# A hybrid encoder trunk on one core: transposes of queries and keys in a new sequence, the closing steps behind the branch, the last products of one output bank postponed

## The reference

```
for layer in range(2):
    hn = rms_norm(x, norm_mix_g[layer])
    z = hn @ w_in                       # x_rnn, y_gate, q, k, v, gates
    # branch 1: depthwise conv, gated linear scan forward and backward, times gelu(y_gate)
    # branch 2: 12 heads in 3 groups, dilated band attention, groups mixed by softmax
    x = x + (sigmoid(g0) * branch_lru + sigmoid(g1) * branch_att) @ w_out
    hn = rms_norm(x, norm_ffn_g[layer])
    if layer == 0: x = x + (silu(hn @ w_gate) * (hn @ w_up)) @ w_down
    else:          x = x + sum over the top 2 of 8 experts of share_e * swiglu_e(hn)
out = rms_norm(x, final_norm_g)
```

## Time and profile before

| | |
|---|---|
| median of 3 runs | 1567.9 us (1566.28 to 1568.82) |
| the profiled execution | 1565.57 us |
| its span, first to last instruction | 1563.8 us |
| PE, DVE, ACT busy | 98%, 53%, 30% of the span |
| DMA | 306 GB/s over the span |
| chain that ended last | PE 82%, ACT 8%, DVE 7%, issue 2% |

### The profile page before, as it was taken

The page is one execution under the profiler, slowest core; times in us unless marked ns, Lnnn a source line. Parts: engine busy times, 40 slices in busy tenths (PEclk is TensorE's granted clock), DMA queues, the critical chain, the costliest instruction groups (busy, mean ns, idle before and its releaser), DMA issues.

```text
span 1563.8 us, 28403 instructions
## 1 busy us (share of the span) xinstructions
PE 1526.8 (98%) x12112; PEld 889.5 (57%) x12112; DVE 822.7 (53%) x1766; ACT 471.7 (30%) x692; POOL 22.9 (1%) x37
## 2 busy tenths in 40 slices
PE   7998999999999989999999999999999999999997
PEld 6886788888888867853434434334334334343342
DVE  6777666555687776754533335336145234342262
ACT  5697655444456977420000000000000000000001
POOL 0000000000000000010000000000000000000000
PEclk9999999999999999999999999999999999999999
DMA  9543265555553433589999999999999999999992
GB/s 384 180 160 136 107 245 200 189 188 189 188 175 135 161 137 123 199 308 413 410 398 425 421 407 425 411 401 425 409 426 418 414 426 411 406 425 413 421 425 109
DMA packets 68354, 478.66 MB, mean 306 GB/s; under 512 B 7616, under 2 KB 7872, under 8 KB 12160
## 3 DMA queue, kind: packets, MB, share of 16 engines
q1 hardware_dynamic: 64480, 460.88, 73.7%
q0 software_dynamic: 3456, 15.72, 2.7%
q10 hardware_dynamic: 288, 0.19, 0.0%
HBM read 471.90 MB, written 4.85 MB: 305 GB/s over the span
## 4 chain that ended last, share of the span: by engine, by line
PE 82%; ACT 8%; DVE 7%; issue 2%; DMA 0%; DVEq 0%; SPq 0%; ACTq 0%
PE bank L1339 26%; PE turn L1354 12%; PE mid L1339 11%; PE turn L1360 6%; PE bank L1076 6%; PE bank L1080 6%; PE bank L1083 6%; ACT w_hi L535 2%; PE mid L1076 2%; PE mid L1083 2%; PE mid L1080 2%; DVE w_lo L542 2%; PE mid L1175 1%; ACT root L890 1%; ACT rg L902 1%
## 5 line engine op out<-in xcount | busy, mean ns | idle before, releaser
L1339 PE MATMUL bank<-wide,gT 128*32 128x512 f32 (+1 forms) x3952 | 423.6, 565 | 0.0
L542 DVE TENSOR_TENSOR w_lo<-raw,w_hi 128x1024 fp32r<-128x1024 f32 x202 | 245.3, 1223 | 142.1 <-ACT w_hi L535 140.0
L1339 PEld LDWEIGHTS bank<-wide,gT 128*32 128x32 f32 x3952 | 154.9, 110 | 245.3 <-issue 238.7
L535 ACT ACTIVATE w_hi<-raw 128x1024 fp32r<-128x1024 f32 x202 | 211.4, 1056 | 122.0 <-PE bank L1083 81.1
L1897 DVE STREAM_TRANSPOSE hT<-eh 32x128 f32<-32x128 f32 (+1 forms) x768 | 219.9, 286 | 24.1
L1354 PE MATMUL turn<-wide,hT 128*32 128x512 f32 x1792 | 215.8, 592 | 0.0
L1339 PE MATMUL mid<-wide,gT 128*32 128x256 f32 (+1 forms) x2048 | 192.0, 486 | 0.0
L1013 ACT ACTIVATE eh<-bank 128x512 f32<-128x512 f32 (+1 forms) x32 | 17.4, 544 | 534.6 <-PE bank L1339 306.3
L1076 PE MATMUL bank<-w_hi,a_hi 128*128 128x512 f32 (+1 forms) x608 | 165.7, 396 | 0.7 <-ACT a_hi L763 0.7
L1083 PE MATMUL bank<-w_lo,a_hi 128*128 128x512 f32 (+1 forms) x608 | 157.4, 383 | 2.1 <-DVE w_lo L542 2.1
L1080 PE MATMUL bank<-w_hi,a_lo 128*128 128x512 f32 (+1 forms) x608 | 157.7, 383 | 0.0
(11 more groups left out here) (254 smaller groups left out, 1165.4 us busy)
## 6 DMA issues: line engine op xcount, KB each, us to landing
wide<-in_stream SPq DMA_DIRECT2D x330, 1024.0 KB, 8.1
raw<-in_stream SPq DMA_DIRECT2D x106, 1024.0 KB, 4.8
wg<-in_gates POOLq DMA_DIRECT2D x2, 2048.0 KB, 10.3
table<-y_rows POOLq DMA_DIRECT2D x7, 384.0 KB, 7.8
gain<-in_norms POOLq DMA_DIRECT2D x4, 512.0 KB, 7.1
x<-in_x SPq DMA_DIRECT2D x2, 512.0 KB, 6.5
raw<-in_stream SPq DMA_DIRECT2D x2, 512.0 KB, 6.8
tokens<-xs POOLq DMA_DIRECT2D x1, 1024.0 KB, 5.4
```

The costliest lines, as they stand in the source:

```text
L535: nc.scalar.activation(w_hi[:, h % H, :], raw[:, part % R, lo:lo + HALF], ACT.Copy).then_inc(hi_ready, 1)
L542: nc.vector.tensor_tensor(w_lo[:, h % H, :], raw[:, part % R, lo:lo + HALF], w_hi[:, h % H, :].bitcast(F32), ALU.subtract).then_inc(lo_rea ...
L1339: ins = nc.tensor.matmul(bank_[strip(s_), 0:w], gT[:, kt, strip(t_)], w_c, start=kt == 0, stop=kt == KT - 1)
```

## The change

1. The `tq` steps run in the sequence 0, 1 / 4, 5 / 2, 3. ACT makes all six copies. Those of 0, 1, 4, 5 wait for the first half of the backward scan only, 2 and 3 for both.
2. `an` stands directly behind `am` (at 20.5 + i, before at 21 + i).
3. The two loads of the first norm's factors (`load_first_gain`) are issued by ACT, the first ahead of the identity and the second behind it; SP issued them before, between the loads of `x` and of the first weights.
4. In the last expert the last three output parts make all their products for `turn[0]` first; then `rows_done` is signalled, and their products for `turn[1]` follow. The strip of `turn[0]` (ACT) and `y_end` (DVE) wait for `rows_done`.
5. The last two products of `ENDS` take `yt` as float32; the steps for high and low words are gone.
6. The closing steps and the last norm stand behind the branch on ACT and DVE, once on each side of it.

```diff
-        at(19.5, ("tq", 2), ("tq", 3))
-        at(20, ("tq", 4), ("tq", 5), ("evac", ("g1", 0)))
+        at(19.5, ("tq", 4), ("tq", 5))
+        at(20, ("tq", 2), ("tq", 3), ("evac", ("g1", 0)))
         for i in range(PAIRS):
-            at(20.5 + i, ("as", i), ("am", i))
-            at(21 + i, ("an", i))
+            at(20.5 + i, ("as", i), ("am", i), ("an", i))
...
             load_x(0)
-            load_first_gain(0)
             sp.dma_start(raw[:, 0, 0:HALF], stream[0, :, 0:HALF]).then_inc(first_landed, 16)
             sp.dma_start(raw[:, 0, HALF:PART], stream[0, :, HALF:PART]).then_inc(landed[0], 16)
             load_x(1)
-            load_first_gain(1)
...
+            load_first_gain(0)
             act.dma_start(const[:, 0:P], consts_in[:, 0:P]).then_inc(s_id, 16)
+            load_first_gain(1)
             act.dma_start(vec[:, :], vecs_in).then_inc(s_vec, 16)
...
-                elif kind == "tq" and s[2] % 2 == 0:
+                elif kind == "tq":
                     idx = TURN[s]
                     bank_full(act, idx)
-                    act.wait_ge(scanned, scans_done(s[1], 1, 1))
+                    act.wait_ge(scanned, scans_done(s[1], 1, int(s[2] in (2, 3))))
...
+            def ends(pas):
+                y0 = outputs_from(pas)
+                ya = 4 * (y0 + EXPERTS)
                 nc.scalar.activation(idle, ident[:, 0:1], ACT.Sqrt).then_inc(idle_s, 1)
-                act.wait_ge(used, u0 + EXPERTS * E_PARTS)
-                ya = 4 * (y0 + EXPERTS)
-                nc.scalar.activation(yt[0:2 * STRIP, :], turn[1][2 * STRIP:P, :], ACT.Copy).then_inc(y_act, 1)
+                if pas == 0:
+                    act.wait_ge(rows_done, 1)
+                else:
+                    act.wait_ge(used, U0 + (pas + 1) * E_LAST)
                 nc.scalar.activation(yt[2 * STRIP:CAP, :], turn[0][CAP:P, :], ACT.Copy).then_inc(y_act, 1)
-                act.wait_ge(y_dve, 3 * (y0 + EXPERTS) + 2)
-                act.wait_ge(y_act, ya + 2)
-                nc.scalar.activation(y_hi[0:CAP, xslice(1)], yt[0:CAP, :], ACT.Copy).then_inc(y_act, 2)
+                act.wait_ge(used, U0 + (pas + 1) * E_LAST)
+                nc.scalar.activation(yt[0:2 * STRIP, :], turn[1][2 * STRIP:P, :], ACT.Copy).then_inc(y_act, 3)
...
             with act.If(most_reg[0] > CAP):
-                experts(1)
-                experts(2)
-            for b in range(TB):
-                act.wait_ge(ms_ready, 2 * DEPTH + b + 1)
-                nc.scalar.activation(sd[:, b:b + 1], ms[:, b:b + 1], ACT.Sqrt).then_inc(sd_ready, 1)
+                ends(0)
+                for pas in (1, 2):
+                    experts(pas)
+                    ends(pas)
+                last_deviation()
+            with act.Else():
+                ends(0)
+                last_deviation()
...
+                            put_off.append((w_, h_, first, last))
+                            if is_last(pas, e) and i >= E_PARTS - PUT_OFF:
+                                if not last:
+                                    continue
+                                ins.then_inc(rows_done, 1)
+                            for w_, h_, first, last in put_off:
+                                for c in range(2):
+                                    n1 = w_[:, c * D + CB:(c + 1) * D]
+                                    for t_ in range(2):
+                                        ins = nc.tensor.matmul(turn[1][strip(2 * c + t_), :],
+                                                               h_[:, c * CAP + STRIP * t_:c * CAP + STRIP * (t_ + 1)],
+                                                               n1, start=first, stop=last)
...
                 pe.wait_ge(y_act, ya + 4)
-                for b, n, place in ENDS[2:]:
-                    nc.tensor.matmul(place, selT[:, b * P:(b + 1) * P], y_hi[:, xslice(n)],
-                                     start=True, stop=False)
                 pe.wait_ge(y_dve, yd + 3)
                 for b, n, place in ENDS[2:]:
-                    nc.tensor.matmul(place, selT[:, b * P:(b + 1) * P], y_lo[:, xslice(n)],
-                                     start=False, stop=True).then_inc(e_turned, 1)
+                    nc.tensor.matmul(place, selT[0:CAP, b * P:(b + 1) * P].bitcast(F32), yt[0:CAP, :],
+                                     start=True, stop=True).then_inc(e_turned, 1)
...
-                elif kind == "tq" and s[2] % 2 == 1:
-                    idx = TURN[s]
-                    bank_full(dve, idx)
-                    dve.wait_ge(scanned, scans_done(s[1], 1, 1))
-                    nc.vector.tensor_copy(qkT[:, s[2], :, :],
-                                          turn[idx % 2][:, :].rearrange("p (a t) -> p a t", a=2)
-                                          ).then_inc(turn_free[idx % 2], 1)
...
+                if pas == 0:
+                    dve.wait_ge(rows_done, 1)
+                else:
+                    dve.wait_ge(used, U0 + (pas + 1) * E_LAST)
+                nc.vector.tensor_copy(y_end[0:CAP, :], turn[0][0:CAP, :]).then_inc(y_dve, 1)
                 dve.wait_ge(used, U0 + (pas + 1) * E_LAST)
-                nc.vector.tensor_copy(y_end[0:CAP, :], turn[0][0:CAP, :]).then_inc(y_dve, 1)
-                dve.wait_ge(y_act, ya + 1)
+                dve.wait_ge(y_act, 4 * (y0 + EXPERTS) + 4)
                 half = yt[0:2 * STRIP, :]
-                nc.vector.tensor_tensor(half, turn[1][0:2 * STRIP, :], half, ALU.add).then_inc(y_dve, 1)
-                add_output(te + 1, *ENDS[0], last)
-                dve.wait_ge(y_act, ya + 4)
-                nc.vector.tensor_tensor(y_lo[0:CAP, xslice(1)], yt[0:CAP, :], y_hi[0:CAP, xslice(1)].bitcast(F32),
-                                        ALU.subtract).then_inc(y_dve, 1)
-                for i in range(1, 4):
+                nc.vector.tensor_tensor(half, turn[1][0:2 * STRIP, :], half, ALU.add).then_inc(y_dve, 2)
+                for i in range(4):
                     add_output(te + i + 1, *ENDS[i], last)
```

More of the change, by code:

```diff
@@ L96 @@
 AT_COMBINE = [2, 2, 4, 4]
+PUT_OFF = 3
 E_TURNS = 4
@@ L1029, in experts, with last_deviation @@
                     square(2 * DEPTH, n, b, xn[:, b, xslice(n)], final_sum)
+            def last_deviation():
+                for b in range(TB):
+                    act.wait_ge(ms_ready, 2 * DEPTH + b + 1)
+                    nc.scalar.activation(sd[:, b:b + 1], ms[:, b:b + 1], ACT.Sqrt).then_inc(sd_ready, 1)
             most_reg = []
@@ L1193, in _ @@
                     if w == 0:
-                        for j in range(4, 6):
+                        for j in range(2, 4):
                             bank_read(pe, TURN[("tq", L, j)])
@@ L1353, in experts @@
                                 for s_, (w_c, t_) in enumerate(((n0, 0), (n0, 1), (n0, 2), (n1, 2))):
[L1354 to L1362 removed]
+                                    ins = nc.tensor.matmul(turn[0][strip(s_), :], h_[:, c * CAP + STRIP * t_:
+                                                                                     c * CAP + STRIP * (t_ + 1)], w_c,
+                                                           start=first and c == 0, stop=last and c == 1)
+                            put_off.append((w_, h_, first, last))
[10 more added lines that the diff above has]
+                                                               n1, start=first, stop=last)
+                                if put_off[-1][1] is not h_:
+                                    ins.then_inc(used, 1)
+                            put_off = []
                         ins.then_inc(used, 1)
@@ L1764, in _, with add_output @@
                                              ALU.mult))
+            def add_output(n, b, half, place, col):
+                dve.wait_ge(e_turned, n)
+                xs_ = x[:, b, xslice(half)]
+                nc.vector.scalar_tensor_tensor(out=xs_, in0=place, scalar=share[:, b, col],
+                                               in1=xs_, op0=ALU.mult, op1=ALU.add).then_inc(summed, 1)
             def experts(pas):
@@ L1823, in add_picked @@
                                 in1=x[:, b, :], op0=ALU.mult, op1=ALU.add).then_inc(picked_added, 1)
-                def add_output(n, b, half, place, col):
-                    dve.wait_ge(e_turned, n)
-                    xs_ = x[:, b, xslice(half)]
-                    nc.vector.scalar_tensor_tensor(out=xs_, in0=place, scalar=share[:, b, col],
-                                                   in1=xs_, op0=ALU.mult, op1=ALU.add).then_inc(summed, 1)
                 c0 = ROUNDS[pas]
@@ L1924, in experts, with last_norm @@
                     dve.wait_ge(final_sum, 4 * (pas + 1))
+            def last_norm():
+                dve.wait_ge(s_gain, 16 * 2 * DEPTH)
+                for b in range(TB):
+                    dve.wait_ge(final_sum, TB + 1 + b)
+                    one = slice(b, b + 1)
+                    link(nc.vector.tensor_tensor(ms[:, one], ss[:, 0, one], ss[:, 1, one], ALU.add))
```

(29 more changed lines are left out.)

24 lines of the change are left out of this document (9 added, 15 removed).

## The result

The changed kernel takes 1548.64 us in the median of four runs (1547.07 to 1550.14), the kernel before 1568.22 beside it: 19.6 us less, a ratio of 0.9877 with the interval 0.986 to 0.9894. The prediction was 1553.3 with a range of 1551.0 to 1557.7.

A forecast was written before the change was run, and what follows sets the result against it. PE was taken to set the pace in the experts, with little room above it, so mixer savings come out at the end. 7.8 + 4.3 + 0 + 2.5 = 14.6 us off 1567.9 gave 1553.3, range 1551.0 to 1557.7.

The forecast's parts named there:

- The slower rival: The 336 expert parts: the DMA stream becomes the bound; at 390 GB/s 38 us are lost, 1591 us; chance 0.03.
- The rival "more than the sum": The start gains its 0.7 us and steps ahead of the attention follow closer: 1552 us or a little less; chance 0.06.
- 1. Transposes: Query/key transposes, both layers: PE's waits for copies go, layer 0's clock stays up; 7.8 us saved, bounds 5.4 to 7.8.
- The wait that I named as late next: Layer 1, half behind the transposes: PE asks for `w_lo` near 565.8, first done by 564.98; 0.8 us of room.
- That the clock would stay up: Layer 0, half behind the query/key transposes: without the waits the clock stays at 2.4 GHz, 0.92 us saved.
- 2. Divisions: Attention rounds: PE's waits for scaled probabilities and two at L1225 go; 4.3 us saved, bounds 0 and 4.3.
- 3. First factors: Start: earlier issue of weights against second factors sharing the DMA engines; 0 us, bounds 0.7 gain and 0.7 loss.
- 4 to 6. The end: Behind the last expert product: shorter closing chain, branch taken in waiting time; 2.5 us saved, bounds 0.4 to 3.0.
- no second jump: End: branch fetch is paid inside waiting time unless a second jump follows on the path; no separate size.
- the half that the prediction names: Layer 0, behind the query/key transposes: 3.77 us against 2.85 in layer 1, 0.92 us expected back.

## Why the prediction was wrong in size

**What bounds the kernel** was right. In the experts PE keeps its 108.21 us for each expert, no part comes late, and what the mixers save comes out at the end to 0.1 us. The slower rival did not occur. The rival "more than the sum" had the direction but not the cause: the start gained nothing.

**1. Transposes.** Expected 7.8, measured 8.1 by distances: 4.70 (4.53 expected) in layer 0, 3.38 (3.25) in layer 1. The wait that I named as late next, for `w_lo`, did not come, and ACT's added copies cost nothing. That the clock would stay up in the stretch of the earlier trace rows was right: 1.00 in each window there. The experiments add that neither of the two edits alone does it: sequence and early waits alone give nothing, the copies alone a little under half by distances (3.4 of 8.1 us).

**2. Divisions: the step that failed.** Expected 4.3, with 4.3 as the upper bound; measured 7.7. I took the idle times of the earlier trace rows as the time lost. They run from the modelled end of the last row, and this lies behind the point at which PE could start the next. The distance shows it: from 588.92 to 590.64 PE needs 1.72 us, in the changed kernel from 577.08 to 577.99 it needs 0.91. That is 0.81 us where the list has 0.65. Three more pieces PE's list of waits has not, or not whole:
- ahead of the first round 580.73 - 579.52 = 1.21 against 0.91, so 0.30, with no wait of PE shown;
- inside each group of transposes the second head's probabilities came later than the first's, hidden in its duration (1.25 against 1.03): 591.82 - 590.64 = 1.18 against 0.97, so 0.21 four times;
- at L1225 614.64 - 613.36 = 1.28 against 1.00, so 0.28 where the list has 0.21.
In a layer 3 x 0.81 + 0.30 + 4 x 0.21 + 0.28 = 3.85 us, and 3.87 were measured. The list of waits of the weight loads (PEld) did show the places that PE's list leaves out, and I had not asked for it:
```profile
PEld turn L1212 <- DVE sm L1686: 9.0, 16, 1.1
```
These are 16 waits, two in each of the eight groups, where PE's list has six; their 9.0 us are more than the 7.1 that PE lost at these groups by the distances above, so that list gives the places and not the size. In part 1 I had measured mostly by distances between starts, and the size was right to 0.3 us; what it missed, 0.17 and 0.13, is near the 0.16 (1.07 less 0.91) by which a modelled end lies late, and part 1 did take the start of the first wait from such an end. The mechanism was right too: the division fits into DVE's idle time, and no split came late.

**3. First factors.** Expected 0 within 0.7; 0.67 us were lost in the first trace, but the changed kernel's second trace is 1 us earlier, and most of the difference is how long the first products run at half rate, a term that the prediction did not have. That the bound of 0.7 held is therefore luck; whether the change costs anything here stays open.

**4 to 6. The end.** Expected 2.5, measured 2.94. Of the miss 0.4 us is there by the first product of the last norm, which DVE begins 5.39 us behind ACT's copy and not 5.8. That the branch is taken in waiting time held, and it carries most. The stall stands where DVE takes the branch on the path, and vanishes where the engine waits anyway; no second jump showed up. The rule of the Trainium skill (Runtime: NRT & Kernel Launch, Instruction fetch mechanics), that a taken branch to a far target has to wait for a fetch of that target, fits this. In the kernel before, a packet of 16 KB on a queue of kind "instruction" moves at 1554.9, just where DVE's idle time begins; that this packet is what DVE waits for isn't shown. The stall's length is not settled by these runs: 2.12 us in one kernel, 3.49 in another.

**From the trace to the median: a second miss, mostly of few runs.** I took the sum, made against the profiled execution, off the median. In this comparison the profiled runs differ by 17.6 us and the medians by 19.6, so 2.0 us of the miss stand here. But the median of before is one of four runs, 1568.22. In the comparisons behind it the kernel before has medians of 1566.65, 1566.81, 1566.23 and 1566.03; all its 74 runs together have 1566.6, and the nine of the changed kernel 1548.2, which is 18.4 us. So 1.2 of the 2.0 us did not come back with more runs, and some 0.8 is left.

For what is left the runs show a cause. The kernel before has waits behind which the granted clock falls in some runs and not in others; its profiled execution held one such fall (1.3 us in layer 0, 0.92 of them in the half that the prediction names), and the mean of five traces with these waits is 1.7. With the waits filled the median falls by 2.5 us and the runs close up. The change takes these falls away together with the waits. I had the first sign of it in hand, the half of 3.77 us in layer 0 against 2.85 in layer 1 under like waits, and counted it as one fixed cost rather than as a chance in each layer and each run.

The miss adds up: 3.4 us from part 2, 0.4 from the end, 0.3 from part 1 and 2.0 between profile and median, less 0.7 at the start, make 5.4. Less 0.4 for the last stores and what lies around the span, and 0.3 because the median of before moved from 1567.9 to 1568.22, that is 4.7. Part 2 alone, put right, would have given 1549.9, inside the spread of the changed kernel's runs.

**Open.** Why single runs of the changed kernel still run at 0.996 and some 4 us longer (two of five, one of four); why the stall of the branch was 3.49 us in one layout; what the first factors' new queue does, and why the first products stay at half rate longer in some executions than in others.

No version beats the changed kernel beyond what a measurement can tell. The nearest is the one with idle products at the start, 1547.75 us in the median.

## What to carry to other kernels

Size a stall of PE by the distance between two starts, against the same pair where nothing stalls, and not by the idle time in a list; waits inside a group of products stand not in PE's list but in that of the weight loads. If a trace shows a fall of the granted clock behind a wait at one place and not at its twin, count it for every such place as something that occurs in a share of the runs, and look at the spread of the runs for its size; compare it over more than four runs. A branch belongs ahead of the last wait of an engine, not behind it.

## What the runs showed of the hardware

- Behind two waits of 1.5 us close together the granted clock fell in five of ten places (five traces, two layers), at a cost of 1.3 to 2.8 us each. With one wait of 3.2 us in their stead eight of ten runs had a mean clock of 0.995 or less, and in the trace the half behind it took 5.2 us rather than 2.85.
- Idle products of 1.4 us in each wait keep it up: the runs' spread falls from 5.8 us to 1.0 but for one run, and the median by 2.5 us.
- At the start the granted clock reads 1.00, and still four products take 2.08 us rather than 1.07, with PE idle until 7.4 us; with idle products from 3.67 us on they take 1.17. Of the 1.2 us gained there 0.25 reach the first query/key transposes.
- A branch that is not entered costs DVE 2.1 to 3.5 us of "issue" where it is on the path (1.9 and 3.2 us from ACT's closing copy to the last product), and nothing that shows where the engine has to wait.
